# Multiplying unscaled rows ahead of the norm's token factor, in a two-block transformer kernel

## The reference, cut to what matters

```python
h = rms_norm(x, norm_mix[l])          # x * rsqrt(mean(x*x) + eps) * gain
z = h @ w_in[l]                       # 2560 columns: q, k, v, recurrence, convolution
q_a = rms_norm(q_a, q_norm[l]); k_a = rms_norm(k_a, k_norm[l])   # per head, then rope
mix = concat([attention(q_a, k_a, v_a), recurrence(...), convolution(...)])
x = x + mix @ w_out[l]
h = rms_norm(x, norm_mlp[l])
x = x + square(relu(h @ w_mlp_in[l])) @ w_mlp_out[l]
```

## Time and profile before

| what | us |
|---|---|
| median of three runs | 3789.46 |
| the three runs | 3782.15, 3790.59, 3789.46 |
| the profiled execution | 3780.52 |
| its span from first to last instruction | 3778.7 |
| PE busy | 3594.5 (95%) |
| DVE busy | 2098.2 (56%) |
| ACT busy | 1398.6 (37%) |

### The profile page before, as it was taken

The page is one execution under the profiler, slowest core; times in us unless marked ns, Lnnn a source line. Parts: engine busy times, 40 slices in busy tenths (PEclk is TensorE's granted clock), DMA queues, the critical chain, the costliest instruction groups (busy, mean ns, idle before and its releaser), DMA issues.

```text
span 3778.7 us, 46927 instructions
## 1 busy us (share of the span) xinstructions
PE 3594.5 (95%) x18482; PEld 2911.0 (77%) x18482; DVE 2098.2 (56%) x2762; ACT 1398.6 (37%) x1873; POOL 872.4 (23%) x716
## 2 busy tenths in 40 slices
PE   8988999998899999999899999999989999989998
PEld 6667888766788878887667888788868778778887
DVE  5867444596744454447667435633574655665434
ACT  4664232366432332123773222222233434332223
POOL 3211655321065536552313640000000000000000
PEclk8999999999999999999899999999999999999999
DMA  5212555421255546663224643233322222223331
GB/s 159 67 51 65 148 148 137 105 71 48 56 153 148 147 110 156 146 144 81 63 68 106 156 129 92 78 99 99 101 76 76 73 76 87 67 62 89 101 90 67
DMA packets 564437, 377.56 MB, mean 100 GB/s; under 512 B 37489, under 2 KB 561354, under 8 KB 564218
## 3 DMA queue, kind: packets, MB, share of 16 engines
q1 hardware_dynamic: 564218, 374.56, 37.6%
HBM read 372.32 MB, written 2.17 MB: 99 GB/s over the span
## 4 chain that ended last, share of the span: by engine, by line
PE 77%; DVE 16%; ACT 4%; issue 2%; SPq 0%; DMA 0%; DVEq 0%; ACTq 0%
PE bank L446 62%; DVE conv_sum L1262 2%; DVE w_lo L424 2%; PE bank L454 2%; PE bank L492 2%; PE bank L865 1%; PE bank L486 1%; PE bank L487 1%; ACT w_hi L415 1%; DVE std L927 1%; DVE norm_tmp L1721 1%; DVE norm_tmp L1715 1%; DVE X L1717 1%; DVE dil_probs L2514 1%; PE bank L2348 1%
## 5 line engine op out<-in xcount | busy, mean ns | idle before, releaser
L446 PE MATMUL bank<-H_hi,w_hi 128*128 128x512 f32 x2384 | 960.2, 403 | 5.4 <-DVE w_lo L424 1.8
L446 PE MATMUL bank<-H_hi,w_lo 128*128 128x512 f32 x2384 | 935.1, 392 | 0.0
L446 PE MATMUL bank<-H_lo,w_hi 128*128 128x512 f32 x2384 | 934.5, 392 | 0.0
L424 DVE TENSOR_TENSOR w_lo<-w_raw,w_hi 128x2048 fp32r<-128x2048 f32 (+3 forms) x285 | 657.7, 2308 | 150.4 <-ACT w_hi L415 141.5
L415 ACT ACTIVATE w_hi<-w_raw 128x2048 fp32r<-128x2048 f32 (+3 forms) x285 | 529.1, 1857 | 305.6 <-DMA w_raw<-in_ffn_w_up 131.0
L525 POOL TENSOR_TENSOR w_mod_raw<-w_mod_raw,silu_c 128x1024 f32<-128x1024 f32 x144 | 282.8, 1964 | 1168.0 <-DMA w_mod_raw<-in_w_mod 1121.7
L446 PEld LDWEIGHTS bank<-H_hi,w_hi 128*128 128x128 f32 x2384 | 449.6, 189 | 131.3 <-issue 38.6
L446 PE MATMUL bank<-U_hi,w_hi 128*128 128x512 f32 x1376 | 540.1, 393 | 4.1 <-DVE note L984 4.1
L446 PE MATMUL bank<-U_hi,w_lo 128*128 128x512 f32 x1376 | 536.4, 390 | 0.0
L446 PE MATMUL bank<-U_lo,w_hi 128*128 128x512 f32 x1376 | 536.3, 390 | 0.0
L446 PEld LDWEIGHTS bank<-H_hi,w_lo 128*128 128x128 f32 x2384 | 449.6, 189 | 96.8 <-issue 0.3
(11 more groups left out here) (370 smaller groups left out, 4603.1 us busy)
## 6 DMA issues: line engine op xcount, KB each, us to landing
w_mod_raw<-in_w_mod SPq DMA_DIRECT2D x576, 128.0 KB, 5.7
w_raw<-in_ffn_w_gate SPq DMA_DIRECT2D x88, 512.0 KB, 4.0
w_raw<-in_ffn_w_up SPq DMA_DIRECT2D x88, 512.0 KB, 5.4
w_raw<-in_dil_w_in SPq DMA_DIRECT2D x36, 1024.0 KB, 5.0
w_raw<-in_w_mlp_in SPq DMA_DIRECT2D x32, 1024.0 KB, 5.9
w_raw<-in_w_mlp_out SPq DMA_DIRECT2D x32, 1024.0 KB, 5.5
w_raw<-in_ffn_w_down SPq DMA_DIRECT2D x32, 1024.0 KB, 5.0
w_raw<-in_w_in SPq DMA_DIRECT2D x16, 1024.0 KB, 5.6
```

The lines of the kernel that those rows point to most:

```text
L424: dve.eng.tensor_tensor(WL[u % SLOTS][:, 0:n], RAW[u % SLOTS][:, 0:n], WH[u % SLOTS][:, 0:n].bitcast(F32), ALU.subtract).then_inc(lo_done. ...
L446: mm = pe.eng.matmul(bank[0:m, :], w[:, k, c0:c0 + m], r[:, k, :], start=(k == 0 and i == 0), stop=(k == kt - 1 and i == 2))
```

## The change

Four norms are rewritten: the mixer's and the MLP's in both layers. The pair multiplies rows that carry the gain but not the token factor (`raw_high` on ACT, `raw_low` on DVE), and `pe_raw_pair` runs sums and spread as jobs between passes of the pair. Behind it ACT and DVE write the fully scaled rows over the same tiles for the remaining units of the stage, each tile as soon as the pair's pass over it is done. The pair's results are multiplied by the factor in bank 5 after they were copied (`z_scaled` for the mixer, `scale_mid` between relu and square for the MLP).

At the start the first two units are not taken side by side but one after the other (`apart`), the bias products come after the fourth pass, the parameter rows are loaded by ACT ahead of its other work, the first two weight units are loaded right behind x, and the tables behind them. `prologue_act_rest` keeps its place behind the rounding of the rows, and the x rows land in another buffer. Core of the diff:

```diff
+        def pe_raw_pair(pe, u, at_pass, apart=False):
...
+            sets = [todo[0:2], todo[2:4]] if apart else [todo]
+            for s, together in enumerate(sets):
+                pe.eng.wait_ge(lo_done.sem, u + (s + 1 if apart else 2))
+                for k in range(DT):
+                    if s == 0:
+                        pe.eng.wait_ge(raw_hi.sem, raw_hi.next(pe))
...
+                    for job in at_pass.get((s, k), ()):
+                        job(pe)
...
+        def mixh_squares(act, l):
...
+            for t in range(4):
+                high(t)
+            square_of(0)
+            square_of(1)
+            for t in range(4, DT):
+                high(t)
+            split_hi(act, lin[("up", l, 0)][2])
+            for t in range(2, DT):
+                square_of(t)
...
+        def raw_high(act, t, gain):
+            act.eng.activation(H[0][:, t, :], X[:, t, :], ACT.Identity, scale=gain(t)).then_inc(raw_hi.sem, raw_hi.add())
...
+        def raw_low(dve, t, gain):
+            dve.eng.wait_ge(raw_hi.sem, raw_hi.next(dve))
+            dve.eng.scalar_tensor_tensor(H[1][:, t, :], X[:, t, :], gain(t), H[0][:, t, :].bitcast(F32), ALU.mult, ALU.subtract).then_inc(raw_lo.sem, raw_lo.add())
...
+        def scaled_high(act, u, ahead_of):
+            for t in range(DT):
+                for job in ahead_of.get(t, ()):
+                    job()
+                act.eng.wait_ge(scaled.sem, scaled.next(act))
+                if t < DT - 1:
+                    act.eng.wait_ge(raw_used.sem, raw_used.next(act))
+                else:
+                    act.eng.wait_ge(acc_ready.sem, units[u + 1]["tiles_end"])
+                act.eng.activation(H[0][:, t, :], NT[2 + t % 2][:], ACT.Identity).then_inc(part_hi.sem, part_hi.add())
...
+        def scaled_tiles(dve, gain, ahead_of):
...
+            for t in range(DT + 1):
+                if t < DT:
+                    ve.scalar_tensor_tensor(NT[2 + t % 2][:], X[:, t, :], gain(t), banks[5][:], ALU.mult, ALU.mult).then_inc(scaled.sem, scaled.add())
...
+                for job in ahead_of.get(t, ()):
+                    job()
+                if t:
...
+                    ve.tensor_tensor(H[1][:, t - 1, :], NT[2 + (t - 1) % 2][:], H[0][:, t - 1, :].bitcast(F32), ALU.subtract).then_inc(rhs_ready.sem, rhs_ready.add())
...
         def last_mix(dve, l):
+            split_lo(dve, u + AHEAD)
             for t in range(DT):
...
+                if t in (4, 5):
+                    raw_low(dve, t - 4, gain)
+            for t in range(2, DT):
+                raw_low(dve, t, gain)
+                add_squares(dve, t - 1)
+            split_lo(dve, lin[("up", l, 0)][2])
+            rstd_column(dve)
...
+            if l == 0:
+                jobs = {(0, 3): [bias_products], (0, DT - 1): [after_bias, pe_running_sums], (1, 0): [pe_spread]}
+            else:
+                jobs = {(0, 0): [pe_running_sums], (0, 1): [pe_spread]}
...
+                act_std(act, D, True)
+                split_hi(act, first + 2)
+                copies = [lambda t=t: z_evac(act, first + t // 2, t % 2, t) for t in range(4)]
+                scaled_high(act, first, {0: copies[0:2]} if l == 0 else {DT - 1: copies[0:2]})
+                for copy in copies[2:4]:
+                    copy()
                 if l == 0:
                     prologue_act_rest(act)
                 mixer_act(act, l)
                 hgrn_act(act, l)
+                mixh_squares(act, l)
+                act_std(act, D, True)
+                scaled_high(act, first, {DT - 1: [lambda j=j: relu_into_mid(act, first, j) for j in range(2)]})
...
+                pe_raw_pair(pe, lin[("up", l, 0)][0], {(0, 3): [pe_running_sums], (0, 4): [pe_spread]})
...
+                rstd_column(dve)
+                split_lo(dve, first + 2)
+                scaled_tiles(dve, lambda t: colp("norm_mix", 8 * l + t), {0: z_jobs[0:2], DT: z_jobs[2:4]} if l == 0 else {DT: z_jobs})
                 if l == 0:
                     prologue_dve_rest(dve)
+                scaled_tiles(dve, lambda t: colp("norm_mlp", 8 * l + t), {DT: [lambda j=j: scale_mid(dve, first, j) for j in range(2)]})
```

More of the change, by code:

```diff
@@ L303, in build @@
             add_units(("z", l), H, specs, "none", acc=(0, 1))
+            units[lin[("z", l)][0]]["waits"] = "tiles"
             add_units(("zv", l), H, [([(0, w[:, 1024:1280])], DT, 256, [tok(0, 256, [0, 1]), tok(0, 256, [2, 3])])], "none", acc=(0, 1))
@@ L310, in build @@
             for q in range(4):
-                add_units(("up", l, q), H, [square(w1, D_FF, 1024 * q + 256 * i) for i in range(4)], "none" if q else "tiles")
+                add_units(("up", l, q), H, [square(w1, D_FF, 1024 * q + 256 * i) for i in range(4)], "none")
+                if q == 0:
+                    units[lin[("up", l, q)][2]]["waits"] = "tiles"
                 add_units(("down", l, q), U, [square(w2[1024 * q:1024 * q + 1024, :], D, 256 * i) for i in range(4)])
@@ L624, in add_products, with running_squares @@
             dve.eng.wait_ge(xy_summed.sem, xy_summed.made)
-        def running_squares(stage, src, ahead=True):
+        def running_squares(stage, src, ahead=True, gain=None):
             def evac(act, u):
@@ L773, in build, with add_to_x @@
         ZQ, ZK, ZV, ZQH, ZFF, ZFB, ZGH, ZA, ZVH = 0, 4, 5, 6, 8, 10, 12, 14, 18
-        def add_to_x(dve, u, stage, squares=False):
+        def add_to_x(dve, u, stage, squares=False, gain=None):
             for j in range(len(units[u]["tiles"])):
@@ L783, in add_to_x @@
                 dve.eng.wait_ge(free.sem, free.made)
+                if gain and t:
+                    raw_low(dve, t - 1, gain)
+                if gain and t == DT - 1:
+                    raw_low(dve, t, gain)
         def pe_mixh(pe, l):
@@ L832, in evac @@
                 n = u - lin[("up", l, q)][0]
+                if q == 0 and n == 1:
+                    for j in range(2):
+                        scale_mid(dve, u, j)
+                    dve_note(dve, rbc_used)
                 for j in range(2):
@@ L1205, in mixer_act @@
             for t in range(4):
-                z_evac(act, first + t // 2, t % 2, t)
-            for t in range(4):
+                act.eng.wait_ge(high_scaled.sem, high_scaled.next(act))
                 head_square(act, t)
@@ L2723, in prologue_pe @@
             mm.then_inc(par_t.sem, par_t.add())
-            pe.eng.wait_ge(fixed_in.sem, fixed_in.next(pe, 16))
-            pe.eng.wait_ge(bias_tab_in.sem, bias_tab_in.next(pe, 48))
-            pe.eng.wait_ge(xt_copied.sem, 5)
-            for g in range(3):
-                mm = te.matmul(banks[BIAS_BANK[g]][0:DIL_HEADS, 0:TOE], BT[:, g * DIL_HEADS:(g + 1) * DIL_HEADS], BO[:, g, :], start=True, stop=True)
-            mm.then_inc(bias_mm.sem, bias_mm.add())
+            pe.eng.wait_ge(xt_copied.sem, DT)
         cols_total = 16 * sum({"q_norm": 2, "k_norm": 2, "c_2": 4}.get(name, 1) for part in TABLE for name, _ in part)
```

177 lines of the change are left out of this document (140 added, 37 removed).

## The result

The changed kernel is slower: 3805.24 us median of four runs (3797.99 to 3810.71) against 3787.49 for the kernel before on the same chip, a ratio of 1.0047 (95% interval 1.0033 to 1.0061). I had forecast 3775, 10.5 us faster. The profiled execution took 3797.99 us (span 3796.2), 17.5 us over the profiled one of before, so the two traces show the difference that the medians show (17.7).

The account below looks back on a forecast made before the run. PE, busy 95% of the span, was taken to bound the kernel. Terms -5.3 - 5.3 - 5.9 + 6 = -10.5 us, from a middle of 3785.8, gave 3775 us; range 3762 to 3788.

Parts of the forecast that it names:

- the path up to the first head sum: Layer one's mixer norm: PE starts 9.2 us before 31.70, the pair ends at 51.6, the first head square comes at 66.1.
- From there to the first q/k spread PE took 11.35 us: Layer one's mixer: the stretch from first head sum to spread keeps 11.35 us, up to 2.4 more after the stall.
- the sum: Whole kernel: -5.3 and -5.3 for the MLP norms, -5.9 for layer two's mixer norm, +6 for the first norm: -10.5 us.
- POOL's later start cost nothing: First layer: earlier weights, tables and later POOL work cost nothing, as the mixer has many us per unit.
- hidden, with 0.1 to 0.5 us to spare; a late square would cost PE one for one: MLP norms: square sums end at 341, PE asks for them at 341.4, so they cause no wait.
- the term for POOL: MLP norms: 0.3 us taken off the 5.6 us gain for DVE's slower operations beside POOL.
- The fourth unit then starts at ... 369.5. Its weights' low part is no earlier: Layer one's MLP norm: fourth unit starts at 369.5 instead of 375.1, its weights' low part ending at 369.4; gain 5.6 us.
- the wait for the bank: MLP norms: the third unit waits 2.5 us for the pair's first bank, freed only behind the seventh scaled tile.
- Layer two's mixer norm: Third unit starts at 718.4 instead of 724.34, after a 1.3 us wait for second-unit weights; gain 5.9 us (4.5 to 7.5).
- The slower rival: Start of the kernel: ACT's parameter issues held up by full queues, x copied 24 us later, net +13.5, 3799 us; chance 0.08.
- The gain is given back: All norms: half clock after new stalls, tile chain beside POOL, 10 us lost in layer one; -1.5, 3784 us; chance 0.23.
- The drain: Table loads on ACT: 1.38 us extra per switch by the page, 4.1 us for three, shrinking the gain to 6.4 us.

Follow-up runs that it names:

- the first mend: Changed kernel with squares ahead of the weight split and square sums ahead of later subtractions in both MLP norms, sums and spread one pass earlier; 3795.03 us, 1.0017.
- the run with filled gaps: Changed kernel with head squares ahead of the tables, plus 13 unread matmuls in PE's idle time ahead of the head sums; 3799.45 us, 1.0038.

## Why the prediction was wrong, step by step

- *First norm, the path up to the first head sum: right.* ACT's issues were over at 10.1 (said 9.7), x's first copy came at 11.66 (11.2), the pair at 24.38 (22 to 23) and its end at 52.4 (51.6; the terms as they stand add up to 51.35), the first head square at 66.64 (66.1). The order on ACT that I read from the code did what I said.
- *First norm, "From there to the first q/k spread PE took 11.35 us", "and up to 2.4 more after an 8 us stall": the step that failed most.* It took 19.91. I saw the stall coming (58.2 to 66.1 said, 59.62 to 67.33 measured) and priced the half clock behind it from the 4.7 us that it had lasted at the pair's begin. It stayed from 61.5 to 85.4, past the last head sum, and cost 8.6 us. Of that the sum holds 0.8 at most (6 us, where the path alone gives 5.2).
- *"POOL's later start cost nothing": wrong, though not in the changed kernel itself.* There the chain came so late (87.94 to 113.17) that it took 25.2 us, as before (25.0); once it came sooner, it met POOL and took 30.5.
- *MLP norms, "hidden, with 0.1 to 0.5 us to spare; a late square would cost PE one for one": the slack was about right, the cover wasn't.* By my own terms the square sums end at 331.2 + 9 = 340.2, not at the 341 that I wrote; with POOL's piece away the twelve operations took 10.3 us, waits for ACT's squares among them, and PE's sums then didn't wait. What failed is the term for POOL, 0.3 us. In the kernel before three subtractions ran beside POOL's piece and took 0.74, 0.87 and 0.86 us instead of 0.69, 0.4 more together; each began with only 0.2 to 0.3 us of the POOL operation beside it left. In the changed kernel two operations began with more than 1 us of it left and lost 2.5 us. PE paid for that not one for one but twice: 2.6 us of waiting and 3.3 of half clock, which accounts for the 5.8 us by which the third unit came later than forecast (32.7 us behind the mixer's output, 26.9 said).
- *MLP norms, "The fourth unit then starts at ... 369.5. Its weights' low part is no earlier": mis-sized.* Even with POOL's piece away the fourth unit came at 42.55 us behind the mixer's output, where I had 39.0.
- *MLP norms, the wait for the bank: right* (2.44 for 2.5).
- *Layer two's mixer norm: right*, including the 1.23 us that PE waits for the second unit's weights (1.3) and the third unit 26.1 us behind the MLP units (26.0 said, 31.9 in the earlier trace rows):

```profile
709.99 0.50 PE L523 MATMUL bank<-H_hi,w_hi 128*128 128x512 f32 x1 [1.23 <-DVE w_lo L428]
...
734.67 0.47 PE L450 MATMUL bank<-H_hi,w_hi 128*128 128x512 f32 x1
```

- *The slower rival* named ACT's issues; they took 0.43 us each, as forecast, and x's first copy came 0.5 us later than said. I had the right sign of a danger in the wrong place. "The gain is given back" came nearer in kind (half clock, tile chain, POOL), but bounded each too low. The drain that it also counts didn't show: the operation behind the second table load began at 66.41, 0.02 us behind the load's end.

What stays open: why the clock fell at head sums with no idle time ahead of them in the first layer (55.74 to 63.88 above), while head sums kept 1.00 in layer two of all 14 traces (in eleven at the same spacing) and in layer one of all five with the old first norm; and whether it falls so in every execution. And whether the new first norm can win at all: with head squares first, sums apart, gaps filled and POOL later the kernel took 3792.64 us, where the one with the old first norm and the same other norms took 3789.16 (1.0016 and 1.0004, intervals overlapping).

## What to carry to other kernels

A step that PE reaches with less than a microsecond to spare is not hidden: ask what else runs then on the engines that feed it, above all POOL beside DVE operations with both operands in SBUF, and put the reserve in by order (squares ahead of subtractions) rather than by hope. Don't price such a meeting by a lucky one: what it costs is what is left of POOL's operation. And don't price the half clock behind a stall by the last one you saw: here the lower clock lasted 4.7 us behind the begin of the first pair, 6.8 behind a stall of 2.6 and 23.9 from within a stall of 7.7. And when a wait goes, look at the next two producers in line; here the fourth unit's weights held back nearly half of what the first mend had freed.

## What the runs showed of the hardware

DVE and POOL disturb each other by the kind of operand. Beside POOL's pieces the subtraction of rows and high part took 2.27 us (0.75 alone), a square sum 1.64 (0.69), a cast 1.88 (0.43), a weight split 2.57 to 2.70 (2.29; 3.87 at 51.08 in the kernel before), and POOL's product 2.39 (mean of all 144: 1.98). The scaling that reads the factor from a bank kept its 0.75 with POOL at work from 338.95 on in the kernel before.

The traces also show how much is lost, and it isn't a factor of two or three. In the 14 traces 1599 operations of DVE on 128x512 with both operands in SBUF began while a POOL operation of 0.3 us or more was running; 1558 of them ended 0.50 to 0.62 us behind the end of that POOL operation, however much of it was left. So they took 0.69 to 2.43 us. Of 1748 with an operand in a bank none took over 0.75. A cheap meeting in the kernel before, DVE and POOL (343.08 behind 342.52):

```profile
342.21 0.87 DVE L722 TENSOR_TENSOR H_lo<-norm_tmp,H_hi 128x512 fp32r<-128x512 f32 x1
```

```profile
340.92 1.60 POOL L527 TENSOR_TENSOR w_mod_raw<-w_mod_raw 128x512 f32<-128x512 f32 x1
```

The Trainium skill (GPSIMD Engine Reference, 1. Specifications) states such contention for DVE instructions with two SBUF inputs; the traces agree, also in what is spared. The cast has one SBUF input only and would have to be of the page's other kind, a 2-port performance mode, which no run here shows.

PE's clock fell at head sums although PE hadn't been idle for 8 us. By the Trainium skill (TensorE: Matmul & The Clock Gate, HAM oscillation — how this bites in real kernels) it is idle gaps of PE that bring the clock down; the run with filled gaps doesn't agree that these alone do. The clock of head sums, from the first to the last of them, was 0.50 to 0.60 in layer one of seven traces with the new first norm and 1.00 in the two with sums apart and gaps filled; that leaves one trace with the gaps alone filled and one with the sums alone apart.
